# Moving a base product over two experts, halving one strip's load, and folding compressed-key scores into score products

## The reference, cut to what matters

```
x = x + expert_choice_ffn(rms_norm(x, norm_ffn[i]), w_router[i], w_gate[i], w_up[i], w_down[i])
g = jax.nn.sigmoid(rms_norm(x, norm_ple[i]) @ w_ple_gate[i])
e = rms_norm(p[i] @ w_ple_proj[i], norm_ple_post[i])
x = x + g * e
```

```
s = jnp.einsum('bsghd,bngd->bghsn', q, kc) * NSA_SCALE
t = jnp.arange(S)
end = jnp.arange(n_cmp) * CMP_STRIDE + CMP_BLOCK - 1
p = masked_softmax(s, end[None, :] <= t[:, None])
o = jnp.einsum('bghsn,bngd->bsghd', p.astype(vc.dtype), vc)
```

## Time and profile before

| what | value |
|---|---|
| median of 3 runs | 1643.87 us (1643.53 to 1644.26) |
| the profiled execution, its own time | 1643.78 us |
| its span | 1642.0 us |
| TensorE busy | 1336.8 us, 81% |
| VectorE busy | 513.8 us, 31% |
| ScalarE busy | 187.8 us, 11% |
| DMA | 518.45 MB, mean 316 GB/s |
| mean granted TensorE clock | 0.921 |

### The profile page before, as it was taken

The page is one execution under the profiler, slowest core; times in us unless marked ns, Lnnn a source line. Parts: engine busy times, 40 slices in busy tenths (PEclk is TensorE's granted clock), DMA queues, the critical chain, the costliest instruction groups (busy, mean ns, idle before and its releaser), DMA issues. The chain is left out here.

```text
span 1642.0 us, 21126 instructions
## 1 busy us (share of the span) xinstructions
PE 1336.8 (81%) x8806; PEld 772.4 (47%) x8806; DVE 513.8 (31%) x1076; ACT 187.8 (11%) x495; POOL 41.2 (3%) x91
## 2 busy tenths in 40 slices
PE   9999676666767655765666679999999999999998
PEld 5553121221113111311122123688888999599953
DVE  3432111111101101100110110445545664467875
ACT  2321010000000000000000000224444000100000
POOL 1100000000000000000000000010000000000001
PEclk9999887887869888988988899999999999999999
DMA  9688999999999999999999999823343441444342
GB/s 400 271 328 363 434 429 428 434 426 431 432 429 435 427 430 435 431 427 433 432 431 427 434 432 424 352 81 120 115 169 118 168 179 66 192 155 154 121 137 101
DMA packets 31492, 518.45 MB, mean 316 GB/s; under 512 B 3524, under 2 KB 4552, under 8 KB 7368
## 3 DMA queue, kind: packets, MB, share of 16 engines
q1 hardware_dynamic: 29360, 514.01, 74.9%
q10 hardware_dynamic: 2072, 3.57, 0.7%
HBM read 515.99 MB, written 1.05 MB: 315 GB/s over the span
## 5 line engine op out<-in xcount | busy, mean ns | idle before, releaser
L1015 PE MATMUL ps<-ring,scr 128*32 128x512 f32 (+3 forms) x3234 | 471.1, 710 | 246.2 <-DMA ring<-in_experts 240.7
L1015 PEld LDWEIGHTS ps<-ring,scr 128*32 128x32 f32 (+2 forms) x3234 | 124.2, 135 | 568.3 <-issue 289.1
L1015 PE MATMUL ps<-turned_T,ring 128*128 128x128 f32 (+1 forms) x1760 | 245.4, 299 | 1.1 <-DVE turned_T L1857 0.8
L1015 PEld LDWEIGHTS ps<-turned_T,ring 128*128 128x128 f32 x1760 | 227.1, 192 | 14.5 <-issue 4.2
L1015 PE MATMUL ps<-scr 128*128 128x128 f32 (+11 forms) x892 | 166.7, 386 | 16.9 <-DVE scr L1986 12.2
L1015 PEld LDWEIGHTS ps<-scr 128*128 128x128 f32 (+4 forms) x892 | 93.9, 177 | 84.2 <-issue 45.5
L1015 PE MATMUL ps<-ring,turned_T 128*128 128x128 f32 (+3 forms) x512 | 128.2, 408 | 0.0
L1015 PEld LDWEIGHTS ps<-ring,turned_T 128*128 128x128 f32 x512 | 82.5, 191 | 42.3 <-issue 30.2
L1989 DVE TENSOR_TENSOR x<-x,ps 128x512 f32<-128x512 f32 x60 | 41.2, 687 | 194.0 <-PE ps L1015 193.9
L1977 DVE SCALAR_TENSOR_TENSOR scr<-scr,ps 128x512 f32<-128x512 f32 x16 | 11.0, 688 | 287.5 <-PE ps L1015 287.5
L1975 DVE SCALAR_TENSOR_TENSOR scr<-scr,ps 128x512 f32<-128x512 f32 x16 | 11.0, 688 | 223.7 <-ACT scr L796 223.7
(11 more groups left out here) (313 smaller groups left out, 1055.5 us busy)
## 6 DMA issues: line engine op xcount, KB each, us to landing
ring<-in_experts SPq DMA_DIRECT2D x69, 4096.0 KB, 23.2
ring<-in_experts SPq DMA_DIRECT2D x48, 2048.0 KB, 21.0
ring<-in_w_ffn_in SPq DMA_DIRECT2D x11, 2048.0 KB, 7.8
ring<-in_w_merge SPq DMA_DIRECT2D x10, 2048.0 KB, 7.9
ring<-in_w_ffn_down SPq DMA_DIRECT2D x11, 1024.0 KB, 4.8
ring<-in_w_out SPq DMA_DIRECT2D x4, 2048.0 KB, 25.5
ring<-in_w_ml SPq DMA_DIRECT2D x4, 2048.0 KB, 8.0
ring<-in_w_nsa SPq DMA_DIRECT2D x4, 2048.0 KB, 8.1
```

Source lines behind the costliest of these rows:

```text
L1015: return pe.matmul(o, l, rr, start=start, stop=stop)
```

## The change

Three things change.

1. `PARTS` ends in 1 instead of 2, and experts 14 and 15 (`LATE`) both have the late form. The base is the x after expert 13. Two of its four products come in expert 14, two in expert 15. The gate weights are loaded with expert 14's strips, and expert 14's down weights are packed in 256-column pieces on the host, as the last one's were.
2. The load of the very last strip is issued as two loads of 1 MB, each with its own semaphore, and TensorE waits for the second only at its eighth step.
3. In the group loop the compressed keys stand in 16 columns ahead of the keys in `kxy`. GpSimd writes them there. The score products of one branch take them along (144 and 272 columns instead of 128 and 256), and the 8 small products are gone. The compressed softmax runs per pair of heads (`compressed_max`, `compressed_exp`, `compressed_probs`), and the transposes of its probabilities come behind the next group's convolution product.

```
-PARTS = (2, 2, 3, 3, 3, 2)
+PARTS = (2, 2, 3, 3, 3, 1)
+LATE = (LAST - 1, LAST)
...
+            for e in LATE:
+                pairs = range(0, 8 if e is LAST else 10, 2)
+                for n in pairs:
+                    s = slots[n]
+                    r.load_two(s, ring[:, s * SLOT:(s + 2) * SLOT], packed["experts"][bass.ds((e * 6 + n // 2) * P, P), :])
+                    if e is not LAST and n == 2:
...
+                    if (e, n) == (LAST, 11):
...
+                        sp.dma_start(dst[:, lower], lead).then_inc(in_lead, 16)
+                        r.load(slots[n], (dst[:, upper], rest))
...
+            def late_y(e, i):
...
+                halves = (e, i) == (LAST, 3)
+                if halves:
+                    pe.wait_ge(in_lead, 32)
...
+                    if halves and k == 8:
+                        arrived(s, 8 + i, True)
...
+            for e in LATE:
...
+                if e is not LAST:
+                    pe.wait_ge(hT_done, 16)
+                    pe.wait_ge(full[9], 144)
+                    gate_product(0, 0)
+                pe.wait_ge(xe_sb, 2 * e + 2)
+                for n in range(8):
+                    gate_up(slots, n)
+                    if e is LAST and n in (1, 5):
+                        gate_product(n // 4, 1)
+                h_turned(e, slots)
+                if e is not LAST:
+                    gate_product(1, 0)
...
+                g_.tensor_copy(kxy[:, :, 0:16], kcall[:, g * 16:(g + 1) * 16].unsqueeze(1).broadcast_to([P, 2, 16]))\
+                  .then_inc(staged, 1)
...
+                            c = slice(keys[t].start - (0 if b else 16), keys[t].stop)
                             ins = mm(bank[2 * par + b][:, c], qs[rows, hp, t * P:(t + 1) * P],
-                                     kxy[rows, b ^ par, 0:(t + 1) * P])
+                                     kxy[rows, b ^ par, 16 if b else 0:16 + (t + 1) * P])
...
+                s, nm = scv[:, :, hp, :, 0:N_CMP], by_pair(nmC, hp)
+                dve.wait_ge(ns_ps, n4 + 2 * hp + 2)
+                chain(dve.tensor_tensor(s, ps[:, 0:4:2, 0:2 * (16 + P)].rearrange("p a (t n) -> p a t n", t=NT)[:, :, :, 0:N_CMP],
+                                        cadd, ALU.add))
+                chain(dve.tensor_reduce(nm, s, AX, ALU.max, negate=True))
+                dve.tensor_tensor(s, s, nm.unsqueeze(3).broadcast_to([P, 2, NT, N_CMP]), ALU.add).then_inc(cs_in, 1)
...
+                compressed_max(n4, g, 0)
                 head_max(n4, 0)
...
-                for hp in range(2):
-                    for t in range(NT):
-                        for par in range(2):
-                            c = 384 + (hp * 2 + t) * 16
...
+                compressed_max(n4, g, 1)
                 head_max(n4, 2)
+                compressed_probs(g, 1)
                 head_max(n4, 3)
```

More of the change, by code:

```diff
@@ L586, in _ @@
             sp.dma_start(slot[9][:, 0:SLOT], a["w_ple_gate"][0]).then_inc(full[9], 16)
[L587 to L595, removed]
+            for e in LATE:
[4 more added lines that the diff above has]
+                    if e is not LAST and n == 2:
+                        sp.wait_ge(e_sq, 2)
+                        sp.dma_start(later[:, 0:SLOT // 2], a["w_ple_gate"][1, :, 0:SLOT // 2]).then_inc(full[6], 16)
+                        sp.dma_start(turned_T[:, KC * T:], a["w_ple_gate"][1, :, SLOT // 2:SLOT]).then_inc(full[7], 16)
+                for n in range(2 * len(pairs), 12):
+                    dst, src = strip_of(slots[n], e, n)
+                    if (e, n) == (LAST, 11):
+                        at = SLOT
+                        src = packed["experts"][bass.ds((e * 6 + n // 2) * P, P), :]
+                        lead = src[:, at:at + SLOT // 2]
+                        rest = src[:, at + SLOT // 2:at + SLOT]
+                        sp.wait_ge(r.free[slots[n]], r.rounds[slots[n]])
+                        sp.dma_start(dst[:, lower], lead).then_inc(in_lead, 16)
+                        r.load(slots[n], (dst[:, upper], rest))
+                    else:
+                        r.load(slots[n], (dst, src))
             r.renamed(TAIL)
@@ L789, in _, with expert @@
             e.then_inc(lg_exp, 1)
-            def expert(e):
+            def expert(e, late=False):
                 act.wait_ge(gt_ps, e + 1)
@@ L1390, in _ @@
             slots = around(ROT)
[L1391 to L1399, removed]
[L1400 to L1405 removed]
+            for e in LATE:
+                if e is LAST:
+                    pe.wait_ge(x_acc, 4 * LAST)
+                gather(e, sele)
+                if e is not LAST:
+                    pe.wait_ge(x_acc, 4 * e)
+                    for h in range(2):
+                        for t in range(NT):
+                            half_turn(x, 4, t, h)
+                gather_turned(e)
+                if e is not LAST:
[8 more added lines that the diff above has]
+                h_turned(e, slots)
+                if e is not LAST:
+                    gate_product(1, 0)
@@ new lines, in _ @@
+                for i in range(4):
+                    late_y(e, i)
+                    late_folded(e, i)
+                    ins = late_gates(e, i)
+                ins.then_inc(fold_ps, 1)
+                pe.wait_ge(fold_sb, 5 * (e - LATE[0]) + 5)
+                for t in range(NT):
+                    for h in range(2):
+                        ins = mm(bank[4 + 2 * t + h], gT[64 * h:64 * h + 64, t * P:(t + 1) * P], zsb[64 * h:64 * h + 64, :],
+                                 e is not LAST and h == 1, e is LAST)
+                        if e is LAST:
+                            ins.then_inc(g_ps, 1)
```

211 lines of the change are left out of this document (94 added, 117 removed).

## The result

The changed kernel takes 1647.32 us (median of 15 runs, 1645.77 to 1648.39); the kernel before took 1643.89 us beside it (15 runs, 1643.41 to 1644.28). The ratio is 1.0020, 95% interval 1.0014 to 1.0027: slower by 0.2%, 3.4 us. The profiled execution took 1647.08 us, its span 1645.3.

What follows compares the result with a forecast made beforehand. Weight arrival was taken to pace the routed experts, TensorE the last expert and the loop. The sum was 1643.8 us + 4.3 (experts) + 0.5 (loop) = 1648.6 us, range 1644.4 to 1651.0.

Steps and rivals of the forecast that it cites:

- Strips 6 and 7 at 961.5 us: Expert 14: gate weights loaded ahead make these strips land 9.7 us later than 951.83, at 961.5 us.
- Second product until 975.5: Expert 14: the second moved base product takes 7.07 us behind the transposes, ending at 975.5 us; 4.2 us are paid.
- Late form 22.2 us: Expert 14: down product in 256-column pieces plus closing products takes 22.2 us, ending at 997.7 us.
- The last expert's 30.8: Last expert, first strip to first down strip: 30.8 us instead of 38.57, without one base product and the DMA wait.
- +4.3: Last expert: its first down strip, and all behind it, comes 4.3 us later, at 1031.1 instead of 1026.84 us.
- The cause: Expert 14: idle time lies before strips 6 and 7 arrive; the second moved product and late form cannot start earlier.
- if strips 6 and 7 ran at 3.64 us: Expert 14: a bound; with these strips at 3.64 us rather than 5.34, the experts' delay would be +2.6 us.
- The loop, "+0.5": Group loop: three groups at -0.23 us each and the fourth at +1.2 make +0.5 us; bounds -3.5 and +2.
- The fourth group, "+1.2": Loop's fourth group: VectorE's chain ends 1.34 us later and holds TensorE's fourth head turn, costing 1.2 us.
- TensorE catches up: Rival, experts: last expert starts before 996 us; 1639.3 us if the loop gives 3.5, otherwise 1643.3; chance 0.10.
- The loop gives all: Rival, group loop: no new ScalarE or fourth-group wait, so -3.5 us there and 1644.6 us total; chance 0.12.
- The clock drop: Rival, expert 14's late form: lower clock or a dry DMA queue costs 2 to 3 us, 1651 to 1652; chance 0.07.

Runs made afterwards that it cites:

- no_halves: The changed kernel with the very last strip loaded in one 2 MB load again; 1647.47 us.
- halves_only: The kernel before with only its very last strip's load split in two; 1643.91 us.
- second_early_warm: The changed kernel with the second base product behind expert 14's second strip, plus 12 useless identity products in each of two later load waits there; 1644.83 us.
- all_warm: The changed kernel with three base products in expert 14, compressed maximum and subtraction behind head 1's maximum, and identity products in three idle times; 1642.80 us.
- second_early: The changed kernel with the second base product moved from behind expert 14's turned h to behind its second strip; 1646.42 us.
- after_warm: The changed kernel, order kept, with 12 useless identity products ahead of expert 14's strips 6 and 7; 1645.54 us.
- experts_only: The kernel before with only the changes to experts 14 and 15 and the split last load, the group loop unchanged; 1647.66 us.
- max_split: The changed kernel with only the compressed add ahead of the first head's maximum; compressed maximum and subtraction come behind the second head's; 1646.40 us.

## Why the prediction was right

The forecast was 1648.6 us, the median is 1647.32, inside the range. Slower by over 0.2% was given 0.74, and it is slower by 0.21%, just beyond that bound; the interval of the ratio reaches to both sides of it, so that this side was met is in part luck. That the kernel got slower, and by which part, is not. By the steps of the prediction:

- **Strips 6 and 7 at 961.5 us**: 961.82. **Transposes done 968.4**: 968.26. **Second product until 975.5**: 975.22. **Late form 22.2 us**: 22.15 (975.22 to 997.37). **Gather 2.6**: 2.58. **The last expert's 30.8**: 30.56 (999.95 to 1030.51). The term "+4.3" measured 3.67: 0.1 to 0.2 us less each in the turned h (1.38 for 1.54), the product's spacing (6.96 for 7.07) and the last expert, none a failed step. Strips 6 and 7 landed 0.3 us late and took 0.3 us less, which cancels by chance. That the last expert waits for no DMA, and that the halves give 0, is shown by the rows and by `no_halves` and `halves_only`. That the last expert's third pair "lands when it did" is not borne out where it can be seen: 1010.34 us in the kernel before, 1012.13 and 1011.97 in `second_early_warm` and `all_warm`. The changed kernel doesn't wait for it.
- **The cause** ("neither the second product nor the late form can start before strips 6 and 7 have arrived") is half of it. Moving the product out of this place (`second_early`) did start the down strips with their landing. What the prediction treated as a bound of one term ("if strips 6 and 7 ran at 3.64 us") was a cause of its own: the row of 5.34 us that I took over is a row partly at the lower clock (the mean over 950 to 960 us is 0.83 in the kernel before). There its excess of 1.7 us was covered by the next load, which came 2.94 us after it; in the changed kernel nothing covers it, and `after_warm` prices it at 1.4 us of the 3.7. What is left fits the product itself: the down strips start 3.68 us behind their landing (975.22 against 971.54, where `second_early` shows it), and 2.25 us of this stay in `after_warm`, at 973.79. That one earlier row gave nearly the right length is luck as well: in the changed kernel's order these strips took 5.06 us in one trace, and 5.07, 5.32 and 6.30 in `experts_only`, `max_split` and `no_halves`.
- **The loop, "+0.5"**: measured -0.25, the one term with the wrong sign. The stall behind ScalarE's copy was right: the memory scores start 6.48 us behind the first scores against 5.80, +0.68 (0.65 forecast). The row behind the small products came 1.10 us closer to the memory scores (0.96 against 2.06), not 1.00. The 32 products behind them got 0.10 us shorter too (3.67 to 3.57), which was not forecast. The two moved transposes were put at the same length in both places: their old place got 0.17 us shorter (0.89 to 0.72), the stretch that they moved into 0.10 longer (5.18 to 5.28). The added columns cost 0.05 us per block as forecast. Together that is -0.50 in the second group against -0.23. The three groups gave -1.28 us where -0.69 was forecast, and the fourth lost 0.17 less than forecast: with the rounding of the sum, the 0.75 us by which the loop was missed.
- **The fourth group, "+1.2"**: +1.03. It was said that its head turn would be held by VectorE; the row at 1274.02 is (0.52 us), and so are the compressed transposes at 1268.39 (0.73 us), which the prediction didn't name. No run separates the two.
- **The rivals**: the first (TensorE catches up) needed the last expert before 996 us, it came at 999.95. "The loop gives all" didn't happen, as the wait of 0.54 us shows. The estimate by the issue floor of about 25 ns in the Trainium skill ("TensorE: Matmul & The Clock Gate", section "Back-to-back issue gap"), by which the 16 records would have been worth 0.4 us, is not borne out: the rows behind them moved up by 1.10 us, 69 ns a record. The same table row of the Trainium skill has about 62 ns per matmul for another way of decoding, by which an estimate gives 1.0 us for the 16; that is near the trace, but no run here shows what sets the pace. The clock drop was priced as a rival in expert 14's late form; there it didn't come (no row above 1.93 us per strip), with a base product just before and no idle time between. It came in `second_early`, which took that product away and left a wait of 2.94 us there.

What stays open: why the changed kernel's runs spread over 2.6 us and those of `second_early_warm` over 0.5. Clocks after waits that differ from execution to execution would do it, and the traces kept bear this out in part. `no_halves` has TensorE's program of the changed kernel up to the very last strip, and in its timeline strips 6 and 7 start with the same landing but take 1.24 us more, all of which reaches the down strips:

```profile
961.87 6.30 PE L1038 MATMUL ps<-ring,scr 128*32 128x512 f32 x32 [3.67 <-DMA ring<-in_experts]
...
976.52 1.93 PE L1038 MATMUL ps<-ring,scr 128*32 128x256 f32 x32
```

No run shows that this is the whole spread. It also means that the 1.4 us of `after_warm` is the price in one pair of executions and not a fixed cost.

## What to carry to other kernels

Idle time of an engine is only worth what can be moved to a place before the wait ends: list for each piece what it depends on, and check on which side of the last arrival it stands. A duration read right behind a wait for a load may be one at the lower clock; if other rows of the same shape are shorter, price both, look at more than one execution, and ask what covers the excess today. Work that is folded into another engine's larger step is free only if nobody waits for that step's start: here three small operations of 0.22 us ahead of a chain made TensorE wait 0.54 us per group, and still 0.25 with two of them behind it.

## What the runs showed of the hardware

The same 32 records (a pair of strips, 128x512 at 32 columns of weights) take 3.64 us where the granted clock is 1.00 (960 to 970 us in `after_warm`), and up to 6.62 us where a part of them runs at the lower level. In expert 14 and the last expert of all these traces, every pair with at most 1.38 us of waiting for a load ahead took 3.64 us, and every pair with 3.17 to 9.36 us took 4.92 to 6.60. Idle time just ahead is not the whole rule. Behind 2.05 to 2.28 us of it both lengths occur, as in expert 14 of `halves_only`:

```profile
922.98 5.23 PE L1020 MATMUL ps<-ring,scr 128*32 128x512 f32 x32 [2.28 <-DMA ring<-in_experts]
...
961.94 3.64 PE L1020 MATMUL ps<-ring,scr 128*32 128x512 f32 x32 [2.25 <-DMA ring<-in_experts]
```

Among the earlier experts one pair of `after_warm`, at 239.82 us, took 3.64 us behind 3.94 us of waiting.

Identity products of 2.9 us that compute nothing, set directly ahead of a load's arrival, were worth 1.4 us (`after_warm`); the same ones with 3.22 us of idle time behind them nothing (`all_warm`). In `second_early_warm` the granted clock over 970 to 980 us was 1.00 instead of the 0.66 of `second_early`. I had not expected the clock to decide what the place of a product is worth: three products in the idle time without fillers ended at 1645.12 us, with them at 1642.80.
